# Hybrid gMLP, stick-breaking and MoE block on one core: the gated branch and its half of the output projection placed between the attention steps

## The reference, cut to what matters

```
h    = rmsnorm(x) * (1 + sc1) + sh1                # sh1, sc1, ga1, sh2, sc2, ga2 = silu(c) @ w_ada + b_ada
proj = h @ w_in                                    # 512 x 2560: u, v (gelu), q, k, vv
o_g  = u * (masked W_s @ layernorm(v) + b_s)       # gMLP branch, 4 groups of 128 channels
o_sb = stick_breaking_attention(q, k, vv)          # 8 heads of 64, causal
x    = x + ga1 * rmsnorm(concat(rmsnorm(o_g), rmsnorm(o_sb)) @ w_out)
h2   = rmsnorm(x) * (1 + sc2) + sh2
y    = experts(h2, top 8 of 64) + shared_expert(h2)
out  = x + ga2 * rmsnorm(y)
```

## Time and profile before

| | |
|---|---|
| median of 3 runs | 1127.2 us (1126.59 to 1131.01) |
| profiled execution, its own time | 1130.07 us |
| its span, first to last instruction | 1128.3 us |
| mean granted TensorE clock | 0.969 |
| PE busy | 1055.3 us of the span |
| DVE / ACT / POOL busy | 749.7 / 569.6 / 514.7 us |

### The profile page before, as it was taken

How to read it: one execution, slowest core, us unless ns; L and a number is a source line. 1 busy time by engine, 2 the same in 40 slices (tenths; PEclk the granted TensorE clock), 3 DMA queues, 4 the chain that set the end, 5 groups by cost and what they waited for, 6 DMA issues and landing times.

```text
span 1128.3 us, 14598 instructions
## 1 busy us (share of the span) xinstructions
PE 1055.3 (94%) x4532; PEld 726.3 (64%) x4532; DVE 749.7 (66%) x1274; ACT 569.6 (50%) x606; POOL 514.7 (46%) x222
## 2 busy tenths in 40 slices
PE   4899997889789999999999999999999999999966
PEld 0687785548554666776677666766676667667622
DVE  1659764743764867777777777777777777677347
ACT  5334235742341655665566556665566556556311
POOL 1233213630330566656665666556655665564100
PEclk9799997989898999999999999999999999999989
DMA  9666742111242699999999999999998889898287
GB/s 343 226 241 259 280 153 65 65 43 62 104 195 88 231 350 351 365 352 374 368 383 358 362 360 353 359 363 366 372 358 334 340 343 346 330 351 349 85 362 307
DMA packets 67911, 318.66 MB, mean 282 GB/s; under 512 B 17136, under 2 KB 17648, under 8 KB 40368
## 3 DMA queue, kind: packets, MB, share of 16 engines
q1 hardware_dynamic: 43152, 269.51, 62.2%
q0 software_dynamic: 22624, 45.40, 11.1%
q10 hardware_dynamic: 2112, 3.45, 0.9%
HBM read 317.25 MB, written 39.85 MB: 316 GB/s over the span
## 4 chain that ended last, share of the span: by engine, by line
PE 81%; DVE 9%; DMA 6%; issue 2%; ACT 2%; SPq 0%; ACTq 0%; DVEq 0%; POOLq 0%; POOL 0%
PE ps L1269 20%; PE ps L1250 11%; PE ps L1252 11%; PE ps L1251 11%; PE ps L963 8%; PE ps L1033 7%; DMA yall<-y_rows 3%; PE ps L1183 3%; PE ps L1158 2%; PE ps L979 1%; PE ps L1089 1%; PE ps L1115 1%; PE ps L1203 1%; DVE acc L1402 1%; DMA ada<-in_w_ada_dram 1%
## 5 line engine op out<-in xcount | busy, mean ns | idle before, releaser
L606 POOL DMA_INDIRECT hg<-h_rows,idxg x70 | 344.1, 4916 | 147.5 <-DVE idxg L1709 145.2
L1715 DVE TENSOR_TENSOR wlo<-raw,whi 128x2048 fp32r<-128x2048 f32 x134 | 300.5, 2282 | 0.0
L841 ACT ACTIVATE whi<-raw 128x2048 fp32r<-128x2048 f32 x136 | 261.3, 1922 | 0.1
L1269 PE MATMUL ps<-rawd,actt 128*128 128x512 f32 x544 | 244.5, 592 | 1.4 <-ACT actt L877 1.4
L1250 PE MATMUL ps<-whi,hthi 128*128 128x512 f32 x544 | 225.3, 414 | 0.0
L1252 PE MATMUL ps<-whi,htlo 128*128 128x512 f32 x544 | 213.0, 392 | 0.0
L1251 PE MATMUL ps<-wlo,hthi 128*128 128x512 f32 x544 | 212.8, 391 | 0.0
L1729 DVE TENSOR_TENSOR htlo<-ps,hthi 128x1024 fp32r<-128x1024 f32 x68 | 83.3, 1225 | 176.6 <-ACT hthi L873 176.6
L883 ACT ACTIVATE ysb<-ps 128x1024 f32<-128x1024 f32 x68 | 69.6, 1024 | 213.5 <-PE ps L1269 213.5
L1269 PEld LDWEIGHTS ps<-rawd,actt 128*128 128x128 f32 x544 | 102.8, 189 | 104.7 <-issue 97.8
L614 POOL DMA_INDIRECT y_rows<-ysb,idxs x68 | 73.3, 1077 | 169.4 <-ACT ysb L883 164.6
(11 more groups left out here) (254 smaller groups left out, 1303.2 us busy)
## 6 DMA issues: line engine op xcount, KB each, us to landing
raw<-in_w_gate_dram SPq DMA_DIRECT2D x68, 1024.0 KB, 8.0
raw<-in_w_up_dram SPq DMA_DIRECT2D x68, 1024.0 KB, 11.1
rawd<-in_w_down_dram SPq DMA_DIRECT2D x68, 1024.0 KB, 13.2
ada<-in_w_ada_dram SPq DMA_DIRECT2D x24, 1024.0 KB, 8.2
yall<-y_rows SPq DMA_DIRECT2D x8, 2048.0 KB, 22.9
wraw<-in_w_in_dram POOLq DMA_DIRECT2D x8, 1024.0 KB, 5.6
woraw<-in_w_out_dram SPq DMA_DIRECT2D x16, 256.0 KB, 2.8
xs<-in_x_dram SPq DMA_DIRECT2D x4, 512.0 KB, 5.7
```

Of the source, the lines that this page charges most:

```text
L606: gp.indirect_dma_start(out=hg[s][:, :, :].rearrange("p k q -> p (k q)"), out_offset=None, in_=h_rows, in_offset=bass.IndirectOffsetOnAxis ...
L841: A(whi[:, s, :, cols], raw[:, s, :, cols], ACT.Copy).then_inc(hi_ok, 1)
L1269: ins = mm(bank(4 + hf), actt[:, k, :], rawd[:, s, k, hf * 512:(hf + 1) * 512], start=(k == 0), stop=(k == KF - 1))
L1715: V.tensor_tensor(wlo[s][:, :, c0:c1], raw[:, s, :, c0:c1], whi[:, s, :, c0:c1].bitcast(F32), ALU.subtract).then_inc(lo_dve, 1)
```

## The change

Nothing is computed differently; the order, the buffers and some operations move.

- The pieces of `w_in` come in the order q, k, vv, v, u. PE runs `project(0)` to `project(7)`, with `modulation_row(2)` to `(5)` after pieces 3, 4, 6 and 7. Then the attention starts. The u projection becomes four `u_chunk(n)` of 24 products.
- PE's step h is now scores(h), filler, transposes(h-1), filler, values(h-1). The fillers are the u chunks (h = 0, 1), `mix` (h = 2), `gated_tr` (h = 3), and the gated half of the output projection as eight `out_g(n)` of 12 products (h = 4 to 7). After attention only `out_s(t)` is left, 24 products a token tile.
- `rest` and `at_sb` lose their second buffer; transposes(h) also wait for both sigmoids of head h+1, and values(h) directly follow transposes(h).
- `w_out` comes as four loads of 1 MB once u is done, without a ring; `wolo` is made in place.
- Two more places for `ada`; load 8 waits for the last transposes of h1. DVE's order between pieces is rewritten.
- The squares of the attention pairs are added on DVE (`sqacc`), and PE sums them once.
- `residual` and `second_norm` multiply by `ga1` and `a2` while ACT takes the squares. `branch_g` is gone.
- `shared_up(0)` and `shared_up(1)` stand between the `h2_transposes`, `shared_up(2)` before `shared_down(0)`. The first loads of gate and up weights are issued after the last h2 rows are stored.

```diff
-        ADA_SLOT = [0, 1, 2, 3, 4, 5, 0, 1] + [n % 2 for n in range(FIRST, 24)]
+        ADA_SLOT = [0, 1, 2, 3, 4, 5, 0, 1] + [6 + n % 2 for n in range(FIRST, 24)]
-        COLG = [DG, 0, 2 * DG, 2 * DG + 512, 2 * DG + 1024]
+        COLG = [2 * DG, 2 * DG + 512, 2 * DG + 1024, DG, 0]
...
-            sp.wait_ge(proj_mm, 4 * PIECES)
-            for n in range(2 * KD):
...
+            sp.wait_ge(u_mm, TT)
+            for j in range(KH):
+                sp.dma_start(woraw[:, 2 * j:2 * j + 2, :], wo_v[:, 2 * j:2 * j + 2, :]).then_inc(wo_in[j], 16)
...
             for t in range(TT):
-                if t == TT - 1:
-                    sp.wait_ge(wo_mm, TT)
-                    load_gate_up(0, 0)
-                    load_gate_up(1, 1)
                 sp.wait_ge(h2_ok, t + 1)
...
+            load_gate_up(0, 0)
+            load_gate_up(1, 1)
             load_down(0, 0)
...
+            def sigmoids(h):
+                ac.wait_ge(z_mm, h + 1)
+                if h >= 2:
+                    ac.wait_ge(att_tr, h - 1)
+                A(beta[:, h % 2], ps[:, 0:1280], ACT.Sigmoid).then_inc(beta_ok, 1)
+                if h >= 1:
+                    ac.wait_ge(att_ok, h)
+                A(rest[:, :], ps[:, 0:1280], ACT.Sigmoid, scale=-1.0).then_inc(beta_ok, 1)
+
+            def weights_out(h):
+                ac.wait_ge(att_tr, h + 1)
+                if h >= 1:
+                    ac.wait_ge(o_mm, h)
+                A(at_sb[:, :], ps[:, AT0:AT0 + 1280], ACT.Copy).then_inc(a_ok, 1)
...
+            sigmoids(3)
             gated_out(0)
             gated_out(1)
-            piece_high(9)
+            weights_out(2)
             gated_out(2)
             gated_out(3)
-
-            for t in range(TT):
-                ins = A(junk[:, 0:DG], u_sb[:, t, :], ACT.Square, accum_out=stat[:, ST_G, t:t + 1])
+            ac.wait_ge(og_ok, GROUPS)
+            for t in range(TT):
+                ins = A(junk_v[:, :], u_sb[:, t, :], ACT.Square, accum_out=stat[:, ST_G, t:t + 1])
                 ins.then_inc(sumsq, 1) if t == TT - 1 else then(ins)
             take_root(ST_G)
+            pair_out(0)
+            for h in range(4, HEADS):
+                n = 2 * (h - 4)
+                sigmoids(h)
+                og_out(n)
+                weights_out(h - 1)
+                og_out(n + 1)
+                if h < 6:
+                    wo_high(h - 2)
+                if h % 2 == 1:
+                    pair_out((h - 3) // 2)
+            weights_out(HEADS - 1)
+            pair_out(3)
...
             for t in range(TT):
-                branch_g(t)
-                if t >= 2:
-                    rows_out(t - 2)
+                squares_s(t)
                 if t >= 1:
                     take_root(ST_O, t - 1, t)
-                squares_s(t)
                 take_root(ST_S, t, t + 1)
-                if t == TT - 1:
-                    rows_out(2)
                 squares_o(t)
+                if t >= 1:
+                    rows_out(t - 1)
...
             def weights_tr(h):
 
                 pe.wait_ge(att_ok, h + 1)
+                pe.wait_ge(beta_ok, min(2 * h + 4, 2 * HEADS))
...
+            def filler(h, part):
+
+                if h < 2:
+                    u_chunk(2 * h + part)
+                elif h == 2:
+                    mix(2 * part)
+                    mix(2 * part + 1)
+                elif h == 3:
+                    gated_tr(2 * part)
+                    gated_tr(2 * part + 1)
+                elif h < HEADS:
+                    out_g(2 * (h - 4) + part)
+
+            for h in range(HEADS + 1):
                 if h < HEADS:
                     scores_mm(h)
+                filler(h, 0)
+                if h >= 1:
                     weights_tr(h - 1)
+                filler(h, 1)
+                if h >= 1:
+                    values_mm(h - 1)
...
+            piece_low(3)
+            weigh(11, 12, 13)
+            piece_low(4)
+            weigh(14, 15)
+            v.wait_ge(row_in, 16 * 7)
+            mod_row(2, ga1, 1, False)
+            piece_low(5)
+            weigh(16, 17)
+            mod_row(3, a2, 2, True)
+            weigh(18, 19)
+            piece_low(6)
+            weigh(20, 21)
+            piece_low(7)
+            weigh(22, 23)
+            mod_row(4, b2, 0, False)
+            piece_low(8)
+            mod_row(5, ga2, 3, False)
+            piece_low(9)
...
+            attend(0)
+            v_norm()
+            attend(1)
+            v.wait_ge(u_ev, TT)
+            gate(0)
+            gate(1)
+            attend(2)
+            gate(2)
+            gate(3)
+            gated_low(0)
+            gated_low(1)
+            attend(3)
             gated_low(2)
             gated_low(3)
             factor(ST_G, DG)
             v.sem_inc(rs_g_ok, 1)
+            pair_low(0)
+            for h in range(4, HEADS):
+                attend(h)
+                if h % 2 == 1:
                     pair_low((h - 3) // 2)
             pair_low(3)
...
             def residual(t):
-                o = o_sb[:, t % 2, :]
+                o = otmp[:, t % 2, :]
+                then(V.tensor_tensor(o, og[:, t, :], ga1[:, :], ALU.mult))
                 factor(ST_S, D, t, t + 1)
```

More of the change, by code:

```diff
@@ L35 @@
 KH = KD // 2
-WO_RING = 3
-ADA_SLOTS = 6
+ADA_SLOTS = 8
 DG = 512
@@ L237, in block_kernel @@
         wplo_pool = sem("wplo_pool")
-        wo_in = [sem(f"wo_in{s}") for s in range(WO_RING)]
+        wo_in = [sem(f"wo_in{s}") for s in range(KH)]
         wohi_ok = sem("wohi_ok")
@@ L767, in _ @@
             piece_high(4)
-            ac.wait_ge(vmean_ok, 1)
-            for t in range(TT):
-                ins = A(junk[:, 0:DG], v_sb[:, t, :], ACT.Square, accum_out=stat[:, ST_V, t:t + 1])
-                ins.then_inc(sumsq, 1) if t == TT - 1 else then(ins)
-            take_root(ST_V)
             evacuate(1)
@@ L780, in _ @@
             evacuate(3)
+            piece_high(9)
+            sigmoids(0)
+            ac.wait_ge(vmean_ok, 1)
+            for t in range(TT):
+                ins = A(junk_v[:, :], v_sb[:, t, :], ACT.Square, accum_out=stat[:, ST_V, t:t + 1])
+                ins.then_inc(sumsq, 1) if t == TT - 1 else then(ins)
+            take_root(ST_V)
+            u_out(0)
+            u_out(1)
+            sigmoids(1)
+            u_out(2)
+            weights_out(0)
+            u_out(3)
+            sigmoids(2)
@@ new lines, in v_norm @@
+            def v_norm():
+                factor(ST_V, DG)
+                for t in range(TT):
+                    then(V.scalar_tensor_tensor(out=v_sb[:, t, :], in0=v_sb[:, t, :],
+                                                scalar=rs[:, ST_V, t:t + 1], in1=lng[:, :],
+                                                op0=ALU.mult, op1=ALU.mult))
+                    ins = V.tensor_tensor(v_sb[:, t, :], v_sb[:, t, :], lnb[:, :], ALU.add)
+                    ins.then_inc(vn_ok, 1) if t == TT - 1 else then(ins)
@@ new lines, in weigh @@
+            def weigh(*pieces):
+                for n in pieces:
+                    weigh_piece(n)
+            piece_low(1)
+            piece_low(2)
+            weigh(8, 9, 10)
+            v.wait_ge(wsp_tr, 1)
+            then(V.tensor_copy(wspt[:, :, :], bank(4).rearrange("p (g q) -> p g q", g=GROUPS)))
+            V.memset(wspt[CHUNK:P, :, 0:CHUNK], 0.0).then_inc(wsp_ok, 1)
+            piece_low(3)
[3 more added lines that the diff above has]
+            v.wait_ge(row_in, 16 * 7)
```

426 lines of the change are left out of this document (190 added, 236 removed).

## The result

The changed kernel takes 1159.5 us (median of 4 runs, 1157.6 to 1162.7) against 1128.9 for the kernel before on the same chip: a ratio of 1.0274, 95% interval 1.0238 to 1.031. The prediction had 1139.5 with a range up to 1150. The sign was right and the size was not: 30.5 us were lost where 12.3 had been worked out. The profiled execution took 1162.7 us, with a span of 1161.0 and a mean clock of 0.959.

A forecast was written before the change was run, and what follows sets the result against it. PE's products bound the expert loop, so shifts of the first expert product move the end: -22.3 projection, +55.5 attention, -13.7 output projection, -1.7 router, -5.5 way into experts: +12.3, 1139.5 us on the median; range 1124 to 1150, forecast's own 1133 to 1146.

The forecast's parts named there:

- Nothing on the path: Way into the experts: later first expert loads and POOL's split, ending some 25 us before needed, cost nothing.
- the wait at piece 6: Projection stage: PE waits 6.1 us for a split behind loads 16 to 19; +7.9 with low clock.
- rival C: Modulation-weight loads slower without a pause, 9.6 instead of 6.5 us a round, about 8 reaching the scores: 1147; chance 0.11.
- Item 4: Attention stage: values of head 4 wait 5.0 us for the second head pair's low part, behind ACT and DVE work.
- Item 1: Attention stage: the first u chunk waits 1.9 us for piece 9, split by ACT, then POOL in 3.44.
- The low clock: Attention stage: slow PE behind five waits at 1.75 us each, 8.8 us in sum.
- the prediction's fifth: Attention stage: low clock, 1.75 us, behind the 1.6 us wait of transposes(2) for both sigmoids of the next head.
- terms of work: Attention stage: PE's products, including the u chunks and gated output fillers, summed to 100.3 us.
- Rival A: Clock holds through the new waits, taking back 13.5 us: 1126, no slower than before; chance 0.17.
- Rival B: Attention filling works: waits under 1 us each, 5 in sum, no clock drop after them: 1110.6; chance 0.12.
- item 3: Attention stage: values of head 2 wait 7.5 us for the first head pair's low part through ACT and DVE.

The follow-up runs named there:

- e6: Changed kernel with the freed-row wait before load slice 18, splits of pieces 4 and 6 ahead of slices, three row loads about 25 us later: 1155.1 us.
- e12: e9 with slices 12 to 23 of the modulation weights loaded by half; read at the first scores alone: 151.67 us, 6.3 sooner.
- e5: Changed kernel with the load queue's wait for the freed norm row, and its load, before slice 18 instead of 16: 1153.0 us, ratio 1.0209.
- e4: Changed kernel with 30, 32 and 8 unused products on PE ahead of the values of heads 2, 4 and 6: 1157.7 us, ratio 1.0244.
- e2: Changed kernel with each head pair's squares, scaling and low part moved ahead of the next head's steps on ACT and DVE: 1137.7 us, ratio 1.0063.
- e9: Changed kernel with the edits of e2 and e5, and the first expert's remainder made by VectorE behind the index tables: 1125.2 us, ratio 0.9945.
- e3: Changed kernel with ACT's two copies of the first expert's high part later, so POOL subtracts after the top-k: 1161.7 us, ratio 1.0286.
- e7: Changed kernel with the first expert's two remainder subtractions on VectorE instead of GpSimd, behind the selection's bf16 copy: 1159.0 us, ratio 1.0257.
- e10: Kernel before with the later row wait in the load queue and the first expert's remainder by VectorE behind the index tables: 1125.3 us, ratio 0.9944.
- e11: e9 with three of the seven 512 KB row loads issued 25 us later: 1127.8 us, ratio 0.9972.

## Why the prediction missed

Two steps failed. The sentence on POOL's split, "Nothing on the path", was wrong in its mechanism. And in the projection stage the wait at piece 6 was put at 6.1 us and took 9.7, and the wait at piece 4 was put at nothing and took 4.7. The attention stage added a third, smaller miss.

**Projection stage (-22.3 predicted, -11.7 measured): a term mis-sized.** The mechanism was right: pieces leave, and piece 6 waits for the slices behind `mod_row(2)`. But the wait was 9.7 instead of 6.1, and there was one of 4.7 us at piece 4 that the sum did not have: together 8.3 of the 10.6 us, and low clock behind piece 4 is part of the rest. The split of piece 4 stands behind slice 13 in the new DVE order; by the prediction's own 9.3 us for that slice, the split would have ended near 96.9 us with PE there at 95.7, so a wait of about 1.2 was due even then (an estimate from the changed kernel's times). Both misses have the same root, the landings. They were taken as 9.3 and 7.6 us from the old order and were 12.6 and 9.1, with 12.9 for the one behind. Between 75 and 83 us the old order issues no slice, and the new one issues one, which itself takes 11.8 us. e6 shows the share of the rows in the first (7.9 with two of the 512 KB rows away), e12 that piece 4's wait is transfer, e5 that the queue's hold for the row of gains cost 7 us of the stage. The prediction named that hold and priced its round trip; that it need not be there it did not ask. Slower loads are rival C, which was 7.5 us above the forecast at a chance of 0.11: its cause came true beside the forecast's, and this stage alone was 10.6 above.

**Attention stage (+55.5 predicted, +61.2 measured): right mechanism, one term short.** The waits were forecast as 1.9, 0.8, 1.6, 7.5, 5.0, 3.2, 1.4 and 2.5 us and measured as 1.68, 0.73, 1.62, 8.23, 8.58, 3.45, 1.33 and 2.78. Seven of eight are within 0.8. They sum to 28.4 against 23.9. Item 4 missed by 3.6, of which 3.3 is the sum of squares that DVE spent behind POOL's remainder of `w_out`. Item 1 came right by luck: it was priced as POOL's 3.44 us for piece 9, which took 2.35, and PE was released by `mod_row(5)` on DVE, 1.8 us late beside POOL. The low clock, 8.8 forecast, with 1.2 behind the sum of squares, is 4 to 8 by e4. Its places were not all right either: the prediction's fifth, behind the wait of 1.6, fell short of its own 1.65, and there the transposes took 1.28 us, the full-clock time. (Its terms of work add to 100.2, not 100.3.) Rival A (the clock holds) is refuted: the windows show 0.88, and the values behind the waits took up to 4.50 us. Rival B (all waits under 1 us, 5 in sum) was wrong for this order; with e2's order the three pair waits are gone, but others of 1.68, 1.62, 1.33 and 2.78 us stay. "The fixed orders on ACT and DVE, which I can only have misjudged in item 3" was the wrong question: the orders were judged well, and they were the fault.

**Output projection, and the router.** 50.6 against 50.4, a period of 10.7 against 10.85; 4.7 against 6.2, since no low clock fell on the router's products in this execution (3.68 us; 6.93 in e9).

**Way into the experts (-5.5 predicted, -1.0 measured): a step that failed.** "POOL's split ends some 25 us before it is needed. Nothing on the path." It asked when the result was needed and not what POOL's work does to DVE. The later loads moved POOL's two subtractions together and onto the top-k. The two stalled steps took 8.7 us where their usual time is 0.6, 8.1 too much; before, one step lost 3.0 us. The difference, 5.1, covers the 4.5 missed. e3 (the stall follows POOL) and e7 (gone without POOL) show the cause. For the step at 253.78 it rests on the trace alone: in e2 the same sum of squares takes 4.09 us where POOL's remainder lies beside it, and 0.69 where none does.

The Trainium skill has this rule, and the prediction did not use it: SBUF — State Buffer ("Who interferes with whom") says that VectorE and GpSimd share a port pair as an exclusive lock, and that a VectorE instruction in a two-port mode, or with both inputs in SBUF while GpSimd reads SBUF, stands until the other has ended. The trace agrees: the stalled forms are a product with both inputs in SBUF (4.32), tensor-scalar (4.36, 4.96) and cast (4.94), and a product with one input in PSUM that began at 364.18, beside POOL's subtraction, took its usual 0.62. And the row for it was in the profile before: 3.44 us for a 0.42 us step, beside POOL's 4.50.

With the sizes measured, the sum is -11.7 + 61.2 - 13.5 - 3.2 - 1.0 = +31.8, against 31.6 at the first expert product.

## What to carry to other kernels

When work is moved between engines' steps, the first question at each new wait is whose turn on the helping engines makes it, and whether that turn can be given to the next consumer first: a pair's two calls on ACT and DVE moved forward gave back 22 us here, and they need no new buffer. A load queue should not wait for a small row in front of large slices that do not need it: in the new order that was 7 us at the first scores, in the old order, where the slices waited for their places anyway, 0.2. Ask of a background GpSimd subtraction which VectorE steps it will lie beside: a result that is ready 25 us early may still have cost the critical engine the whole of its duration. What worked here was to let VectorE make it in time in which it waits (e9). And a rearrangement is to be held against the old order with the same mends: e9 beat the kernel before, and e10 equalled e9.

## What the runs showed that I had not expected

- VectorE instructions of 0.18 to 0.6 us last 4.3 to 5.0 when they fall into the start of GpSimd's 4.5 us subtraction. Not every form does: in the kernel before, MAX8 and MATCH_REPLACE8 steps of 0.2 to 0.6 us ran at their usual length beside POOL's subtraction at 333.92, and the step that stood 3.44 us was a comparison with both inputs in SBUF. GpSimd keeps its pace: 9.16 and 9.18 us for two in a row beside the stalled steps, 4.50 for one in the kernel before.
- VectorE does the same subtraction, 128x2048, in about 2.3 us where GpSimd takes 4.5.
- A 1 MB slice that lands in 5.1 us at best took 12.6 in company of the rows and 7.9 without two of them; half a slice landed in 3.6. Delaying the rows then made the later slices slower (e6, e11).
